# Index scores moved between the k steps of two projection tiles, and rotations moved ahead of and into the top-k search

## The reference, cut to what matters

```python
u = jnp.einsum('bsd,de->bse', h, w_in[layer])
q, k, v, z_attn, q_idx, k_idx, w_idx, z_ssd, xbc, dt_raw = _split_cols(u, IN_WIDTHS_2)
q = _rope_partial(q.reshape(bsz, seq, ATTN_Q_HEADS, ATTN_HEAD_DIM), pos)
k = _rope_partial(k.reshape(bsz, seq, ATTN_KV_HEADS, ATTN_HEAD_DIM), pos)
...
logits = jax.nn.relu(jnp.einsum('bqhd,bsd->bqhs', qib.astype(jnp.float32), k_idx32))
score = jnp.einsum('bqhs,bqh->bqs', logits, wb.astype(jnp.float32))
score = jnp.where(admissible[None], score, -jnp.inf)
_, sel = lax.top_k(score, topk)
...
s = jnp.where(valid[:, :, None, None, :], s, -jnp.inf)
p = jax.nn.softmax(s, axis=-1).astype(vg.dtype)
```

## Time and profile before

| what | value |
|---|---|
| median of 3 runs | 1828.46 us (1828.44 to 1828.81) |
| the profiled execution's own time | 1829.15 us |
| its span, first to last instruction | 1827.4 us |
| PE busy | 1764.4 us, 97% of the span |
| DVE, ACT, POOL busy | 1002.7, 574.9, 714.4 us |
| mean granted PE clock | 0.991 of full speed |

### The profile page before, as it was taken

One profiled execution on the slowest core, in us unless ns is written; L12 is line 12 of the kernel. 1 busy time (PEld: TensorE's weight loads), 2 busy tenths in 40 slices (PEclk: granted clock), 3 DMA queues, 4 the chain that ended last, 5 costly groups with the idle time before them and its releaser, 6 DMA issues.

```text
span 1827.4 us, 22151 instructions
## 1 busy us (share of the span) xinstructions
PE 1764.4 (97%) x7938; PEld 1415.2 (77%) x7938; DVE 1002.7 (55%) x1382; ACT 574.9 (31%) x796; POOL 714.4 (39%) x303
## 2 busy tenths in 40 slices
PE   7999999999999999999899999999989999999996
PEld 6877778788888887888778777777748777778885
DVE  4344333333322645113678989897599766576326
ACT  5322222322222224123632333333362323251211
POOL 3433333343444444443344324343314333325445
PEclk9999999999999999999899999999999999999998
DMA  5322222222333323332433222232212222217422
GB/s 200 114 81 81 81 82 92 81 81 81 99 103 92 97 95 131 116 126 69 163 93 114 69 70 93 62 88 81 69 36 92 81 69 69 80 58 252 126 83 92
DMA packets 50091, 175.55 MB, mean 96 GB/s; under 512 B 5217, under 2 KB 5473, under 8 KB 48865
## 3 DMA queue, kind: packets, MB, share of 16 engines
q1 hardware_dynamic: 41472, 152.13, 26.8%
q10 hardware_dynamic: 8544, 22.37, 3.4%
HBM read 166.09 MB, written 8.39 MB: 95 GB/s over the span
## 4 chain that ended last, share of the span: by engine, by line
PE 75%; DVE 20%; ACT 2%; issue 2%; POOL 1%; DMA 0%; ACTq 0%; DVEq 0%; SPq 0%; POOLq 0%
PE bank L330 73%; DVE gate L1065 3%; DVE feats L1053 2%; DVE bias L1053 2%; DVE bias L1553 1%; PE bank L334 1%; DVE top L1549 1%; DVE probs L1053 1%; DVE gT L1415 1%; DVE gate L1097 1%; DVE nmax L1092 1%; DVE tmp L1053 1%; DVE probs L1104 1%; DVE wide L1408 1%; POOL w_lo L308 1%
## 5 line engine op out<-in xcount | busy, mean ns | idle before, releaser
L308 POOL TENSOR_TENSOR w_lo<-raw,w_hi 128x1024 fp32r<-128x1024 f32 x280 | 688.8, 2464 | 1096.7 <-ACT w_hi L718 1096.7
L330 PE MATMUL bank<-planes_hi,w_hi 128*128 128x512 f32 (+1 forms) x1792 | 709.7, 396 | 19.0 <-DVE w_lo L1128 9.4
L330 PE MATMUL bank<-planes_lo,w_hi 128*128 128x512 f32 (+1 forms) x1792 | 694.8, 388 | 0.0
L330 PE MATMUL bank<-planes_hi,w_lo 128*128 128x512 f32 (+1 forms) x1776 | 687.7, 387 | 0.0
L718 ACT ACTIVATE w_hi<-raw 128x1024 fp32r<-128x1024 f32 x280 | 296.9, 1060 | 909.6 <-PE bank L330 893.3
L330 PEld LDWEIGHTS bank<-planes_hi,w_hi 128*128 128x128 f32 x1792 | 339.7, 190 | 110.2 <-issue 36.6
L330 PEld LDWEIGHTS bank<-planes_lo,w_hi 128*128 128x128 f32 x1792 | 340.1, 190 | 70.2 <-issue 4.8
L330 PEld LDWEIGHTS bank<-planes_hi,w_lo 128*128 128x128 f32 x1776 | 336.2, 189 | 68.3
L330 PE MATMUL bank<-w_hi,planes_hi 128*128 128x512 f32 x512 | 199.9, 391 | 4.2 <-DVE planes_lo L1069 4.2
L330 PE MATMUL bank<-w_hi,planes_lo 128*128 128x512 f32 x512 | 199.2, 389 | 0.0
L330 PE MATMUL bank<-w_lo,planes_hi 128*128 128x512 f32 x512 | 199.2, 389 | 0.0
(11 more groups left out here) (252 smaller groups left out, 1376.5 us busy)
## 6 DMA issues: line engine op xcount, KB each, us to landing
raw<-in_stream SPq DMA_DIRECT2D x282, 512.0 KB, 3.6
h_rows<-feats ACTq DMA_DIRECT2D x4, 1024.0 KB, 7.0
feats<-in_x_t SPq DMA_DIRECT2D x3, 1024.0 KB, 10.5
bias<-in_x_rows ACTq DMA_DIRECT2D x2, 1024.0 KB, 6.2
probs<-in_x_rows ACTq DMA_DIRECT2D x2, 1024.0 KB, 8.4
bias<-h_rows ACTq DMA_DIRECT2D x2, 1024.0 KB, 6.7
probs<-h_rows ACTq DMA_DIRECT2D x2, 1024.0 KB, 8.0
out<-feats ACTq DMA_DIRECT2D x6, 256.0 KB, 2.9
```

Of the source, the lines that this page charges most:

```text
L308: nc.gpsimd.tensor_sub(w_lo[:, s, :], raw[:, s, :], w_hi[:, s, :].bitcast(fp32)).then_inc(lo_ready, 1)
L330: return nc.tensor.matmul(o, a, b, start=start, stop=stop)
```

## The change

The diff has three parts. First, `project` gets a table `after`, which says what to run after a given k step; the old argument `between` is expressed by it. The signal that a unit of weights is used up stays at the unit's last k step, ahead of what runs after it. Second, the eight calls of `idx_scores` are no longer one stretch ahead of `T_KV` 0: four of them run after k steps 3, 7, 11 and 15 of `T_KV` 0, and four after the same steps of `T_KV` 1. ACT's list is reordered to match: for each of the two tiles relu 4k, the rounding of the first unit, relu 4k+1 and 4k+2, the rounding of the second unit, the copy of the accumulator, relu 4k+3. Third, on DVE the two rotations of k stand ahead of the search, and the rotation of the first head's q stands ahead of round 6 of its 16 rounds. No computation is added or removed.

```diff
-                    last.then_inc(unit_used, 1)
-                    if u == 0 and between is not None:
-                        between()
+                        if k == UK - 1:
+                            last.then_inc(unit_used, 1)
+                        if e in after:
+                            after[e]()
...
-            for t in range(8):
-                idx_scores(t)
-            project(tile_at(T_KV, 0), T_KV - SK - 1)
-            for t in range(1, 4):
+            def idx_after(first):
+                return {4 * n + 3: lambda t=first + n: idx_scores(t) for n in range(4)}
+
+            project(tile_at(T_KV, 0), T_KV - SK - 1, after=idx_after(0))
+            project(tile_at(T_KV, 1), T_KV + 1 - SK - 1, after=idx_after(4))
+            for t in range(2, 4):
                 project(tile_at(T_KV, t), T_KV + t - SK - 1)
...
-            for t in range(8):
-                relu_scores(t)
-            for k, dst in enumerate((kT[:, 0, :], kT[:, 1, :], feats[:, 2, :], feats[:, 3, :])):
+            for k, dst in enumerate((kT[:, 0, :], kT[:, 1, :])):
+                m, p = tile_at(T_KV, k)
+                relu_scores(4 * k)
+                round_unit(m + 1, 2 * p)
+                relu_scores(4 * k + 1)
+                relu_scores(4 * k + 2)
+                round_unit(m + 1, 2 * p + 1)
+                take((m, p), dst, T_KV - SK + k + 1)
+                relu_scores(4 * k + 3)
+            for k, dst in ((2, feats[:, 2, :]), (3, feats[:, 3, :])):
...
+            dve.wait_ge(rope_q_loaded, 16)
+            dve.wait_ge(acc_taken, T_KV - SK + 2)
+            rope(kT[:, 0, :], kT[:, 0, :], P, rope_q, swap16, None, 0, padded[:, 16:16 + S])
+            rope(kT[:, 1, :], kT[:, 1, :], P, rope_q, swap16, k_roped, 1, padded[:, 16:16 + S])
+
+            def rope_head(h):
+                dve.wait_ge(acc_taken, T_HEAD2 - SK + 2 * h + 1)
+                rope(qT, tmp, P, rope_q, swap16, q_roped, h + 1, padded[:, 16:16 + S])
+
             for i in range(1, QB):
                 step(V.memset(bias[0:64, i, P * i + 64:P * i + P], INADMISSIBLE))
 
             for r in range(TOPK // 8):
+                if r == 6:
+                    rope_head(0)
...
-            dve.wait_ge(rope_q_loaded, 16)
-            dve.wait_ge(acc_taken, T_KV - SK + 2)
-            rope(kT[:, 0, :], kT[:, 0, :], P, rope_q, swap16, None, 0, padded[:, 16:16 + S])
-            rope(kT[:, 1, :], kT[:, 1, :], P, rope_q, swap16, k_roped, 1, padded[:, 16:16 + S])
...
-            rope_head(0)
```

More of the change, by code:

```diff
@@ L352, in project_first, with project @@
                 last.then_inc(unit_used, 2)
-            def project(tile, acc_before, planes_cut=None, between=None):
+            def project(tile, acc_before, planes_cut=None, after={}):
                 m, p = tile
@@ L445, in _ @@
             project(tile_at(T_HEAD1, 1), None)
-            project(tile_at(T_HEAD1, 2), 2, between=turn_cum)
-            project(tile_at(T_HEAD1, 3), 3, between=lambda: turn_and_spread(0))
+            project(tile_at(T_HEAD1, 2), 2, after={UK - 1: turn_cum})
+            project(tile_at(T_HEAD1, 3), 3, after={UK - 1: lambda: turn_and_spread(0)})
             for h in range(1, HEADS):
@@ L457, in _ @@
                 attn_pv1(a)
-                project(tile_at(T_HEAD1, 4 * h + 3), first + 2, between=lambda: turn_and_spread(h))
+                project(tile_at(T_HEAD1, 4 * h + 3), first + 2, after={UK - 1: lambda: turn_and_spread(h)})
             a = HEADS - 1
@@ L1560, in _ @@
             step(V.memset(bias[0:64, 0, 64:P], BIG))
-            dve.wait_ge(rope_q_loaded, 16)
-            dve.wait_ge(acc_taken, T_KV - SK + 2)
-            rope(kT[:, 0, :], kT[:, 0, :], P, rope_q, swap16, None, 0, padded[:, 16:16 + S])
-            rope(kT[:, 1, :], kT[:, 1, :], P, rope_q, swap16, k_roped, 1, padded[:, 16:16 + S])
-            def rope_head(h):
-                dve.wait_ge(acc_taken, T_HEAD2 - SK + 2 * h + 1)
-                rope(qT, tmp, P, rope_q, swap16, q_roped, h + 1, padded[:, 16:16 + S])
-            rope_head(0)
             with step.loop(1, HEADS, 17) as h:
```

## The result

The changed kernel takes 1837.68 us (median of 5 runs, 1837.38 to 1840.26), the kernel before 1828.46 us in the same comparison (1827.79 to 1828.82). The ratio is 1.0053, with a 95% interval of 1.0042 to 1.0063: 9.2 us slower. The forecast was 1838.5, in a range from 1834.0 to 1842.5.

The account below looks back on a forecast made before the run. The prediction took DVE's stretch from the sums to the first softmax to set the pace, with PE waiting for it. Later softmax +8.7, earlier projection -0.65 and cold clock +2.0 gave +10.0 us: 1838.5 us, range 1834.0 to 1842.5.

Parts of the forecast that it names:

- Step 1: On PE, a burst of scores between projections costs 2.33 us with entry and exit, bounds 1.92 to 4.25.
- Step 2: On PE, eight cheaper bursts let `T_HEAD2` 0 end at 1399.57 instead of 1411.54, 11.97 us ahead.
- Step 3: On DVE, the sums of the scores end at 1370.9 instead of 1363.04, with about 7.8 us idle in pieces.
- Step 4: On DVE, k's two rotations cost 6.4 to 9.8 us; with six search rounds, round 6 comes between 1395.6 and 1399.0.
- Step 5: DVE waits at least 2.5 us for the first q; first softmax at 1436.9 instead of 1428.20, 8.7 us later.
- Step 6: First softmax to last scaled probability stays 14.24 us; projection follows 0.46 behind instead of 1.11, returning 0.65 us.
- Step 7: Behind PE's long idle at the first head, the lowered clock costs 2.0 us, bounds 0 and 2.5.
- The sum: Whole kernel: later softmax, earlier projection behind the probabilities and lowered clock together make it 10.0 us slower.
- (a): Rival: PE sets the end, so its gains at the scores and first head count, 1812.3 us; chance 0.03.
- (b): Rival: a burst's halves do not overlap, 4.25 us each, 1853.9 us; chance 0.05, shared with more than one late step.
- (d): Rival: no change, PE's later slack swallows the later softmax, 1828.5 us; chance 0.03.
- (c): Rival: no meeting with POOL (-2.6), warm clock (-2.0), 1833.9 us; chance 0.13, including values up to the forecast.

Follow-up runs that it names:

- PE kept at work: Changed kernel plus 100 additional 128 x 512 matmuls into an unused bank, in PE's wait ahead of the first head's transposes: 1836.42 us.
- the scores alone: Changed kernel with the three rotations put back behind the search, the scores still between the k steps: 1831.82 us.
- late k rotations: Changed kernel with the two rotations of k ahead of round 14 and that of the first q ahead of round 10: 1831.32 us.
- dense scores: Changed kernel with score tile 0 ahead of `T_KV` 0, one tile after every second k step of it, and all rotations behind the search: 1828.82 us.
- early gate: Kernel with dense scores, all three rotations ahead of round 14, and the gate's sigmoid left ahead of the scaling of the probabilities: 1829.51 us.
- the late one: Kernel with dense scores, all three rotations ahead of round 14, and the gate's sigmoid moved behind the scaling of the probabilities: 1817.75 us.

## Why the prediction was right, point by point

All its positions are shifted by the 1.30 us at the copy, which belong to no step.

- **Step 1, a burst costs 2.33 us: right.** 2.33 measured at the first burst, 2.37 as the mean by their distance (5.09 less 2.72 for four k steps). The changes between matmuls of 64 and of 128 rows thus cost no more than the 0.41 to 0.45 us of entry and exit together.
- **Step 2, `T_HEAD2` 0 ends at 1399.57: right.** 1398.27 after the shift, 1398.52 measured.
- **Step 3, the sums end at 1370.9: the mechanism right, a term missing.** 1369.6 after the shift, 1370.96 measured. Missing is POOL: a sum, too, is stretched when it starts in a subtraction (1.60 instead of 0.48). I had applied that to the rotations only, since no sum before had a subtraction beside it.
- **Step 4, k and six rounds: above the bound.** The two rotations took 10.2 us, against 6.4 to 9.8: in each the sum was stretched to 2.8 us, where the step had gone by a product of 2.18.
- **Step 5, a wait of at least 2.5 us at q, softmax at 1436.9: the wait mis-sized, the end right.** The sign named for it, an idle time of 2 to 6 us, did not come. The misses of steps 3 and 4 used up the wait: 0.84 us were left. Because q's copy set the start of the rotation, neither miss reached the end: 1435.6 after the shift, 1435.91 measured. Had they been a microsecond larger, they would have; that much of the end's accuracy is luck.
- **Step 6, 14.24 us and a return of 0.65: right together, by two small misses.** 13.76 measured, two subtractions back to back as foreseen; but projection follows 0.82 behind the last probability (1450.49 against 1449.67) and not 0.46, so that 0.29 came back and not 0.65.
- **Step 7, 2.0 us for the clock: right in kind and about right in size.** The granted clock was 0.50 until 1454. Between the first projection behind the transposes and the end 1.6 us were lost; with PE kept at work 1.3 (medians) to 1.9 us (from the copy) went away.
- **The sum**, +8.7 - 0.65 + 2.0 = +10.0, stands against +9.0 - 0.8 + 1.6 = +9.8 in the profiles and +9.2 in the medians. Of the rivals, (a), PE sets the end, is refuted by the run with 100 matmuls more; (b) by the burst of 2.33; (d) by the result; of (c), neither part came.

What the prediction did not see is how its own sum is made up. It read the +8.7 at the softmax as idle time of DVE, 7.8 of it in the sums, with DVE's work the same. In the profile DVE idles 3.6 us in the sums and 0.84 at q, and its busy time on the page has grown by 4.7 (1002.7 to 1007.4): POOL's subtractions stretch four sums by 5.7 together, where they stretched none before. In the sums the first three stretches change nothing at the end, since DVE waits for later scores all the same; what sets the end is when the last scores come, plus the last stretch of 1.1. Between the parts of the change the runs divide the loss thus: the late sums cost 9.2 us with their stretched instruction, but the interleaving alone costs only 3.6, since it also clears POOL from the rotations; moving the rotations forward, where they meet POOL, and where PE's cold restart is exposed, costs the other 5.9 (1837.68 less 1831.82). Of these 5.9, 5.1 are there at the start of the first softmax (109.39 us from the copy against 104.29 with the scores alone), so they are DVE's rotations and its wait at q; the rest lies behind it, where the clock is. No run times the two apart with precision; late k rotations gave back 6.4, the busy PE 1.3.

## What to carry to other kernels

Before filling the waits of the busiest engine, find the engine that it waits for, and ask whether the new order feeds that one as densely as the old. Spreading work evenly over PE's steps (5.09 us apart) starved an engine that takes 3.91 us a portion. An edit can be worth nothing alone and something beside another one: under the dense scores the rotations at round 14 changed nothing with the early gate (1829.51 against 1828.82) and gained 6.0 us with the late one (1817.75 against 1823.72), because `head_turn` waits for two arrivals and both had to move.

## What the runs showed of the hardware that I had not expected

- A scalar_tensor_tensor of 128 x 512 with two SBUF inputs is held by POOL's subtraction like a tensor_tensor: 2.77 us instead of 0.75. In the kernel before, the search's max and match_replace ran beside nine subtractions without a trace of it, 2.97 us a round throughout.
- The same three rotations behind the search took 9.1 us with no subtraction beside them and 14.7 with three instructions held (10.8 with one).
- After the wait of 24.2 us the granted clock was 0.50, the lower level of 1.2 GHz, until 1454, some 6 us after the first transpose, while 4.2 us of idling before the change was followed by about 4 us of lowered clock.
